# Sparse heads of the even attention: the selection mask is added to the bias bands by GpSimd, not by sixteen products with the identity

## The chip, the cores and the metric

The kernel runs on one core of a Trainium2 chip. The metric is the device time of one execution in microseconds, the median of three runs. Engines: PE is TensorE, DVE is VectorE, ACT is ScalarE, POOL is GpSimd, SP is SyncE, which here only issues weight transfers. PSUM is the memory TensorE writes into, SBUF the memory all engines read; GpSimd doesn't touch PSUM in this kernel.

## The reference

Two transformer blocks of two layers each run in turn over 256 tokens of width 1024. The second block's layer 0 is the "even" layer. Its mixer has two kinds of heads: four differential heads (eight softmaxes) and eight sparse heads, called DSA, which may only see the 64 keys that an index score ranks highest for each query:

```python
    act = jax.nn.relu(jnp.einsum('bqhd,bsd->bqhs', qi, k_idx))
    score = jnp.einsum('bqhs,bqh->bqs', act, wi)
    score = jnp.where(adm[None], score, -jnp.inf)
    _, sel = lax.top_k(score, topk)                     # topk = 64
    ...
    bias = table_a[t5_bucket(sel - tpos[None, :, None])]
    s = jnp.einsum('bqhl,bqkl->bqkh', ql, c_sel) * scale + bias
    s = jnp.where(valid[..., None], s, NEG_INF)
    p = jax.nn.softmax(s, axis=2)
```

The kernel does not gather keys. It computes the scores against all keys and makes the excluded ones so large (the scores are kept negated, so "large" is 1e30) that their exponential is zero. One selection per query serves all eight sparse heads.

## The kernel before

**Tiling.** Tokens lie in two tiles of 128 queries (`qt` 0 and 1). Under the causal limit a query tile 0 sees 128 keys and a query tile 1 sees 256. A "unit" is one head and one query tile. The even layer has 32 units, taken in eight steps `s` of four (two heads by two query tiles): steps 0 to 3 are the differential heads ("joint"), steps 4 to 7 the sparse ones.

**What a unit goes through.** TensorE multiplies queries and keys into PSUM (`scores`). VectorE adds the head's bias band, writes the result to SBUF and takes the row minimum in the same instruction (`biased`, two records on VectorE). ScalarE takes the exponential and its sum. For the differential heads VectorE then combines two softmaxes (`joined`). TensorE transposes the weights (`turn`), VectorE or ScalarE copies them out of PSUM (`copied`), and TensorE multiplies them with the values. Every engine follows a fixed written order and semaphores: `at_s` says that a unit's scores are there, `at_t` that its bias is added, `at_e` that its exponential is done, `at_joint`, `at_x`, `at_yd` and `at_ya` follow for joining, transposing and copying, `at_o` for the values.

**How the mask gets in.** VectorE ranks the index scores in eight rounds of "eight largest" and "replace them" per query tile (`top_rounds`); the last line writes a bf16 tile `sel`, 1e30 where a key is not selected, 0 elsewhere, and counts `sel_ready`. TensorE adds `sel` to the scores of a sparse unit in PSUM by a second product, identity times `sel` (line 1847). Only these second products count `at_s`, so VectorE may not start on any unit of a sparse step before all its query-key products have been issued.

**Around it.** While steps 0 to 3 run, TensorE also computes the last 200 columns of the layer's input projection (`in2_half`, 128x200 products), whose weights VectorE and ScalarE split in two parts (`whi`, a cast by ScalarE, line 2152; `wlo`, a subtraction by VectorE, line 2737). At step 6 VectorE takes the differential heads' output (`diff_out`, `diff_total`, lines 3461 to 3470) and GpSimd normalises it (lines 1042 to 1058).

**Memory.** `band` is the first 4096 columns of `region`, 16 heads by 256 columns; the even layer uses 12. `proj[:, :, 640:1152]` held the index queries, which are dead once they have been transposed; so is `qiT`, `region[:, 3072:4096]`, once the index scores are computed.

Of the kernel before, what the change touches and what calls it, by code (L numbers as in the profile page):

```python
# [204 lines left out]
def build_network(nc, a, out):  # L205
# [66 lines left out]
    with ExitStack() as ctx:  # L272
# [29 lines left out]
        sel = sb("sel", [P, 3 * P], BF16)  # L302
# [19 lines left out]
        cand = region[:, 7040:7296], work[:, 2560:2816]  # L322
# [147 lines left out]
        sel_ready = sem("sel_ready")  # L470
        diff_taken = sem("diff_taken")
# [32 lines left out]
        def unit(qt, slot, w, parts, bias, pv, o_bank, o_col, sel_mask=None):  # L504
            return dict(qt=qt, slot=slot, w=w, parts=parts, bias=bias, pv=pv, o_bank=o_bank, o_col=o_col, sel=sel_mask)
# [19 lines left out]
        def head_unit(qt, q, k, nk_of, bias, v, slot, o, masked):  # L525
            nk = nk_of(qt)
            return unit(qt, slot, nk, [(0, nk, q(qt), k(nk))], bias(qt, nk), [v(s) for s in range(nk // P)], *o(qt),
                        sel[:, (0, P)[qt]:(0, P)[qt] + nk] if masked else None)
# [18 lines left out]

        def even_heads():
            hs = []
            for i in range(2 * HB):  # L550
# [3 lines left out]
                           lambda s, i=i: proj[:, s, 2248 + P * (i // 2):2248 + P * (i // 2) + P], i, out_at(P * (i // 2)), False))  # L554
            return hs

        def dsa_heads():
            hs = []
            for i in range(HA):
                b = half(i)  # L560
                hs.append((lambda qt, i=i, b=b: qT[b:b + 64, 8 + i // 2, qt * P:qt * P + P],
                           lambda nk, i=i, b=b: qT[b:b + 64, 12 + i // 2, 0:nk], causal, band_of(i),
                           lambda s, i=i: proj[:, s, HD * i:HD * i + HD], 2 * HB + i, out_beside(i), True))
            return hs

        def odd_heads():
            hs = []
            for i in range(HC):
# [3 lines left out]
                           lambda s, kv=kv: proj[:, s, 1152 + HD * kv:1152 + HD * kv + HD], i, out_columns(i), False))  # L572
            return hs

        def cross_heads():
            hs = []
            for i in range(HX):
# [3 lines left out]
                           lambda s, i=i: kvn[:, s, 256 + HD * i:256 + HD * i + HD], i, lambda qt, i=i: (6 + qt, P * (i // 2)), False))  # L581
# [341 lines left out]
        def _(pool):  # L923
# [105 lines left out]
            for l in range(DEPTH):  # L1029
# [86 lines left out]
        def _(pe):  # L1116
# [259 lines left out]
            def attention_steps(key):  # L1376
# [3 lines left out]
                def scores(i):  # L1380
# [18 lines left out]
                    for (c0, n, q, k), (c1, _, q1, k1) in zip(pair[0][1]["parts"], pair[1][1]["parts"]):  # L1399
                        m0 = nc.tensor.matmul(scores_of(*pair[0])[:, c0:c0 + n], q, k, start=True, stop=pair[0][1]["sel"] is None)  # L1400
                        m1 = nc.tensor.matmul(scores_of(*pair[1])[:, c1:c1 + n], q1, k1, start=True, stop=pair[1][1]["sel"] is None)
                    if pair[0][1]["sel"] is not None:
                        m0, m1 = [nc.tensor.matmul(scores_of(u, d), ident_b[:], d["sel"], start=False, stop=True) for u, d in pair]
# [107 lines left out]
            for _ in range(WARM):  # L1511
                nc.tensor.matmul(ps[:, 0, :], sel[:, 0:P], sel[:, 0:P].unsqueeze(1).to_broadcast([P, 4, P]), start=True, stop=True)
# [211 lines left out]
            for l in range(DEPTH):  # L1724
# [97 lines left out]
                if even:  # L1822
# [8 lines left out]
                    def scores(s):  # L1831

                        fours = [(u0 + 4 * s + j, us[4 * s + j]) for j in range(4)]
                        for qt in range(TT):
# [1952 lines left out]
```

## Time and profile before

| | |
|---|---|
| time, median of 3 runs | 1346.65 us (1346.65 to 1347.08) |
| span of the profiled execution | 1344.9 us |
| median minus span (start and end around it) | 1.75 us |
| busy in the span: PE, DVE, ACT, POOL | 1334.0, 974.7, 740.4, 124.2 us |
| the last ranking result is written | 788.7 us after the span's start |
| sparse steps, first scores to last values | 799.3 to 817.2 us |
| sixteen products with the identity | 800.2 to 809.5 us |

The times of rows are microseconds from the span's start. The profiled execution gives durations and their order; its span is 1.75 us shorter than the median of the timed runs, so a difference worked out in the trace is added to the median. The timeline lists an instruction's start and duration; consecutive instructions on an engine overlap a little (an end is drawn after the next start), so what one costs its engine is best read from start to start.

### The profile page before, as it was taken

What the parts mean: (1) busy time and instruction counts of PE and PEld (TensorE: products, weight loads), DVE (VectorE), ACT (ScalarE), POOL (GpSimd) and SP (SyncE); (2) the same over time, 40 slices, a digit from 0 to 9 for tenths busy, and PEclk for the clock granted to TensorE, in tenths of its full rate; (3) what the DMA queues carried; (4) which work ended last, traced back from release to release, by engine and by line L of the source; (5) the groups of instructions that cost most, each with busy time, mean ns of one, the idle gap of its engine ahead of it and who ended that gap; (6) DMA issues with size and microseconds to landing.
All of it is one profiled execution on the core that took longest, in us unless ns stands there. A gap on an engine that the chain in (4) does not pass through costs nothing.

```text
span 1344.9 us, 19217 instructions
## 1 busy us (share of the span) xinstructions
PE 1334.0 (99%) x7365; PEld 1121.8 (83%) x7365; DVE 974.7 (72%) x1502; ACT 740.4 (55%) x1155; POOL 124.2 (9%) x114
## 2 busy tenths in 40 slices
PE   9999999999999999999999999999999999999998
PEld 6888888888888888888888777888888878888886
DVE  7566878777664767877778787886667887786665
ACT  6564555454545754555455676754445675654443
POOL 1000011111000000311111002220000011400000
PEclk9999999999999999999999999999999999999999
DMA  9743545555455334667655523357765524355552
GB/s 374 247 151 131 188 157 190 189 193 194 173 219 188 125 126 161 227 200 232 202 190 198 172 95 149 119 217 223 218 206 191 183 79 173 122 203 193 191 190 89
DMA packets 37673, 244.32 MB, mean 182 GB/s; under 512 B 4656, under 2 KB 5312, under 8 KB 10192
## 3 DMA queue, kind: packets, MB, share of 16 engines
q1 hardware_dynamic: 33568, 228.08, 47.5%
q0 software_dynamic: 3728, 14.82, 4.1%
q8 instruction: 59, 0.97, 0.3%
q14 instruction: 30, 0.25, 0.1%
q10 hardware_dynamic: 288, 0.21, 0.1%
HBM read 241.13 MB, written 1.97 MB: 181 GB/s over the span
## 4 chain that ended last, share of the span: by engine, by line
PE 97%; ACT 1%; DVE 1%; DMA 0%; issue 0%; POOL 0%; ACTq 0%; DVEq 0%
PE ps L1217 19%; PE ps L1155 17%; PE ps L1161 16%; PE ps L1164 16%; PE ps L1224 10%; PE ps L1323 3%; PE ps L1449 2%; PE ps L1418 2%; PE ps L1400 1%; PE ps L2035 1%; PE ps L1265 1%; PE ps L1262 1%; PE ps L1259 1%; PE ps L1577 1%; PE ps L2045 1%; PE ps L1578 1%
## 5 line engine op out<-in xcount | busy, mean ns | idle before, releaser
L2737 DVE TENSOR_TENSOR wlo<-raw,whi 128x1024 fp32r<-128x1024 f32 (+2 forms) x423 | 510.4, 1217 | 264.1 <-ACT whi L2152 263.2
L2152 ACT CAST whi<-raw 128x1024 fp32r<-128x1024 f32 (+1 forms) x431 | 444.5, 1041 | 332.5 <-PE ps L1224 188.5
L1217 PE MATMUL ps<-act,whi 128*128 128x512 f32 x1120 | 266.4, 390 | 0.0
L1217 PEld LDWEIGHTS ps<-act,whi 128*128 128x128 f32 x1120 | 208.4, 188 | 42.2
L1155 PE MATMUL ps<-whi,mhi 128*128 128x512 f32 (+2 forms) x688 | 235.7, 392 | 0.0
L1161 PE MATMUL ps<-wlo,mhi 128*128 128x512 f32 (+2 forms) x688 | 231.1, 385 | 0.0
L1164 PE MATMUL ps<-whi,mlo 128*128 128x512 f32 (+2 forms) x688 | 230.9, 385 | 0.0
L1164 PEld LDWEIGHTS ps<-whi,mlo 128*128 128x128 f32 x688 | 129.3, 188 | 26.3
L1161 PEld LDWEIGHTS ps<-wlo,mhi 128*128 128x128 f32 x688 | 129.2, 188 | 26.0 <-DVE wlo L2737 0.5
L1224 PEld LDWEIGHTS ps<-act,wlo 128*128 128x128 f32 x1120 | 143.6, 191 | 5.5
L1155 PEld LDWEIGHTS ps<-whi,mhi 128*128 128x128 f32 x688 | 125.9, 188 | 23.8 <-issue 2.6
L1224 PE MATMUL ps<-act,wlo 128*128 128x256 f32 x1120 | 145.3, 283 | 0.0
L1155 PE MATMUL ps<-whi,act 128*128 128x512 f32 (+1 forms) x336 | 126.3, 376 | 0.0
L1164 PE MATMUL ps<-whi,act 128*128 128x512 f32 (+1 forms) x336 | 124.1, 369 | 0.0
L1161 PE MATMUL ps<-wlo,act 128*128 128x512 f32 (+1 forms) x336 | 124.0, 369 | 0.0
L1155 PEld LDWEIGHTS ps<-whi,act 128*128 128x128 f32 x336 | 63.3, 188 | 11.6 <-ACT whi L2152 0.8
L1164 PEld LDWEIGHTS ps<-whi,act 128*128 128x128 f32 x336 | 63.3, 188 | 10.9
L1005 POOL TENSOR_TENSOR work<-work 128x512 f32<-128x512 f32 x22 | 48.4, 2199 | 257.8 <-DVE work L3139 250.0
L1161 PEld LDWEIGHTS ps<-wlo,act 128*128 128x128 f32 x336 | 63.4, 189 | 10.1
L939 POOL TENSOR_TENSOR rstd<-ss,small 128x2 f32<-128x2 f32 (+1 forms) x22 | 19.3, 878 | 492.7 <-DVE ss L3289 166.8
L2215 ACT ACTIVATE work<-work,low 128x128 f32<-128x128 f32 (+3 forms) x80 | 40.8, 512 | 28.4 <-DVE low L2831 24.1
L2692 ACT CAST mhi<-work 128x512 fp32r<-128x512 f32 x32 | 19.9, 622 | 66.0 <-DVE work L3739 66.0
(334 smaller groups left out, 1516.2 us busy)
## 6 DMA issues: line engine op xcount, KB each, us to landing
raw<-in_weights SPq DMA_DIRECT2D x210, 1024.0 KB, 4.8
gain_b<-in_norm_g POOLq DMA_DIRECT2D x6, 512.0 KB, 4.1
raw<-in_weights SPq DMA_DIRECT2D x5, 512.0 KB, 6.0
region<-in_b_gate POOLq DMA_DIRECT2D x2, 1024.0 KB, 8.2
o_nat<-in_mem_turned POOLq DMA_DIRECT2D x2, 1024.0 KB, 6.8
region<-band POOLq DMA_DIRECT2D x8, 256.0 KB, 5.0
region<-band POOLq DMA_DIRECT2D x8, 192.0 KB, 6.3
x<-in_x SPq DMA_DIRECT2D x1, 1024.0 KB, 11.9
```

The costliest lines, as they stand in the source:

```text
L1005: nc.gpsimd.tensor_tensor(two(up_as), two(up_a), row, ALU.mult).then_inc(a_scaled, 1)
L1155: nc.tensor.matmul(o, hi[:, kx, rows_], wh[:, k, c0:c0 + w], start=first and h == 0 and k == 0 and (tt == 0 or at[1] == 0), stop=False)
L1161: nc.tensor.matmul(o, hi[:, kx, rows_], wl[:, k, c0:c0 + w], start=False, stop=False)
L1164: mm = nc.tensor.matmul(o, lo[:, kx, rows_], wh[:, k, c0:c0 + w], start=False, stop=final and h == 1 and k == kh - 1 and (tt == 1 or at[1] ...
L1217: nc.tensor.matmul(ps[:, bank0 + f, :], of(whi, h)[:, k, f * P:f * P + P], act2[:, kx].rearrange("p i n -> p (i n)"), start=kx == 0, stop= ...
L1224: mm = nc.tensor.matmul(ps[:, bank0 + f, 0:SEQ], of(wlo, h)[:, k, f * P:f * P + P], act2[:, kx, 0], start=False, stop=kx == KD - 1)
L1323: mm = nc.tensor.transpose(bank[:, j * P:j * P + P], src, ident)
L1418: mm = nc.tensor.transpose(turned(u, d)[:, at:at + P], step_of(1536, u, d)[:, at:at + P], ident)
L1449: mm = nc.tensor.matmul(ps[row:row + HD, d["o_bank"], d["o_col"]:d["o_col"] + P], d["pv"][b], values_of(u, d)[:, b * P:(b + 1) * P], start ...
L2152: nc.scalar.copy(whi[:, m % HL, 0:w], raw[:, n % RAW, h * w:h * w + w]).then_inc(hi_done, 1)
L2215: nc.scalar.activation(step_of(1536, u, d), step_of(0, u, d), ACT.Exp, scale=-1.0, bias=low[:, d["qt"], s:s + 1], accum_out=den[:, d["qt"] ...
L2737: nc.vector.tensor_tensor(wlo[:, m % HL, 0:w], raw[:, n % RAW, h * w:h * w + w], whi[:, m % HL, 0:w].bitcast(F32), ALU.subtract).then_inc( ...
```

## The change

The tile `sel` is gone. VectorE writes the mask as f32 into dead parts of `region` (`out_of_top`). GpSimd, whose queue holds nothing between the norm of the latent keys and the wait for `diff_taken`, adds it to the eight sparse heads' bands: for query tile 0 into a copy in the dead part of `proj` (two instructions of four heads by 128), for query tile 1 in place in `band` (four instructions of two heads by 256). VectorE reads these masked bands in `biased`, with one more wait, `masked_ready`. TensorE's second products go, and each query-key product now counts `at_s` itself. The constant tile of the warm-up products at the program's start gets a name of its own, `warm`.

```diff
-        sel = sb("sel", [P, 3 * P], BF16)
+        warm = sb("warm", [P, P], BF16)
...
-        cand = region[:, 7040:7296], work[:, 2560:2816]
+        cand = region[:, 7040:7168], work[:, 2560:2816]
+        out_of_top = region[:, 7168:7296], region[:, 3072:3328]
...
+        def first_masked(h0, n=1):
+
+            return proj[:, h0 // 4, 640 + P * (h0 % 4):640 + P * (h0 % 4 + n)]
+
+        def masked_of(h):
+            return lambda qt, nk: band[:, h, :] if qt else first_masked(h)
...
                     root(("ckv", l), 2)
+
+                    pool.wait_ge(sel_ready, TT * (l // 2) + 1)
+                    for h in (0, 4):
+                        nc.gpsimd.tensor_tensor(first_masked(h, 4).rearrange("p (h n) -> p h n", n=P), band[:, h:h + 4, P:SEQ],
+                                                out_of_top[0].unsqueeze(1).to_broadcast([P, 4, P]), ALU.add).then_inc(masked_ready, 1)
+                    pool.wait_ge(sel_ready, TT * (l // 2) + 2)
+                    pool.wait_ge(masked_ready, (HA // 2 + 2) * (l // 2) + 2)
+                    for h in range(0, HA, 2):
+                        pair = band[:, h:h + 2, :]
+                        nc.gpsimd.tensor_tensor(pair, pair, out_of_top[1].unsqueeze(1).to_broadcast([P, 2, SEQ]), ALU.add).then_inc(masked_ready, 1)
...
                             pe.wait_ge(at_t, u0 + 4 * s - (0 if qt or not s else 2))
-                            mms = []
                             for u, d in pair:
                                 (_, _, q, k), = d["parts"]
-                                mms.append(nc.tensor.matmul(scores_of(u, d), q, k, start=True, stop=d["sel"] is None))
-                            if pair[0][1]["joint"]:
-                                for mm in mms:
-                                    mm.then_inc(at_s, 1)
-                        if not fours[0][1]["joint"]:
-                            for u, d in fours:
-                                nc.tensor.matmul(scores_of(u, d), ident_b[:], d["sel"], start=False, stop=True).then_inc(at_s, 1)
+                                nc.tensor.matmul(scores_of(u, d), q, k, start=True, stop=True).then_inc(at_s, 1)
...
-                    pe.wait_ge(sel_ready, TT)
...
+                    if d["pair"] is not None and not d["joint"]:
+                        dve.wait_ge(masked_ready, (HA // 2 + 2) * (key[1] // 2) + (2 + d["pair"] - HB + 1 if d["qt"] else (d["pair"] - HB) // 2 + 1))
...
-                        nc.vector.tensor_scalar(sel[:, (0, P)[qt]:(0, P)[qt] + nk], c, SENTINEL / 2, BIG, ALU.is_gt, ALU.mult).then_inc(sel_ready, 1)
+                        nc.vector.tensor_scalar(out_of_top[qt], c, SENTINEL / 2, BIG, ALU.is_gt, ALU.mult).then_inc(sel_ready, 1)
```

On TensorE, at the first two sparse steps (4 and 5), the queue before holds the query-key products (`ps<-qT`), the mask products (`ps<-sel,ident_b`) and the transposes of steps 2 and 3 (`ps<-cst,work`):

```order
L1841 MATMUL ps<-qT 128x128 [waits at_t,sel_ready]
L1841 MATMUL ps<-qT 128x128
L1841 MATMUL ps<-qT 128x256 [waits at_t]
L1841 MATMUL ps<-qT 128x256
L1847 MATMUL ps<-sel,ident_b 128x128 x2
L1847 MATMUL ps<-sel,ident_b 128x256 x2
L1428 MATMUL ps<-cst,work 128x128 [waits at_ya,at_joint] x2
L1428 MATMUL ps<-cst,work 128x128
L1841 MATMUL ps<-qT 128x128 [waits at_t,ev_act]
```

and after the change:

```order
L1856 MATMUL ps<-qT 128x128 [waits at_t]
L1856 MATMUL ps<-qT 128x128
L1856 MATMUL ps<-qT 128x256 [waits at_t]
L1856 MATMUL ps<-qT 128x256
L1444 MATMUL ps<-cst,work 128x128 [waits at_ya,at_joint] x2
L1444 MATMUL ps<-cst,work 128x128
L1856 MATMUL ps<-qT 128x128 [waits at_t,ev_act]
```

The four mask products of the step are gone, and the transposes follow the scores directly; nothing else moves on TensorE.

On GpSimd, between the norm of the latent keys (`rstd<-ss,small`) and the squares of the differential heads' output (`o_nat<-o_nat`), the queue before is:

```order
L1027 DMA work<-in_ev_a_w_uk 128x4x128
L1028 DMA work<-in_ev_a_w_uv 128x8x64
L939 TENSOR_TENSOR rstd<-ss,small 128x2 [waits ss_ready]
L1042 TENSOR_TENSOR o_nat<-o_nat 128x512 [waits diff_taken] x2
L1048 COPY work<-rden 128x512 [waits at_x,dsa_weights]
```

and after the change:

```order
L947 TENSOR_TENSOR rstd<-ss,small 128x2 [waits ss_ready]
L1048 TENSOR_TENSOR proj<-region 128x512 [waits sel_ready]
L1048 TENSOR_TENSOR proj<-region 128x512
L1054 TENSOR_TENSOR region<-region 128x512 [waits masked_ready,sel_ready]
L1054 TENSOR_TENSOR region<-region 128x512 x3
L1060 TENSOR_TENSOR o_nat<-o_nat 128x512 [waits diff_taken] x2
L1066 COPY work<-rden 128x512 [waits at_x,dsa_weights]
```

Six additions stand ahead of the squares, behind the transfers of that part. On VectorE the order of the instructions is the same; the sixteen sparse `biased` instructions each have one wait more.

## Rows read from the trace of the kernel before

**Rows 1.** The page's first part: engine, busy us (share) x instructions.

```profile
PE 1334.0 (99%) x7365; PEld 1121.8 (83%) x7365; DVE 974.7 (72%) x1502; ACT 740.4 (55%) x1155; POOL 124.2 (9%) x114
```

**Rows 2.** Windows: length, busy PE, PEld, DVE, ACT, POOL, granted clock, DMA, GB/s.

```profile
794.86:805.24 10.38, 10.18 (x90) 8.45 (x89) 8.68 (x43) 10.38 (x40) 0.00 (x0) 1.00 0.01 2
805.24:812.17 6.93, 5.66 (x55) 4.11 (x54) 6.61 (x28) 5.56 (x19) 5.03 (x6) 1.00 0.00 1
812.17:840.00 27.83, 27.82 (x160) 23.00 (x161) 18.41 (x22) 15.54 (x23) 2.22 (x3) 1.00 0.45 170
```

**Rows 3.** Line 1847, the mask products: durations, and who waited for them.

```profile
L1847 PE MATMUL ps<-sel,ident_b x16: 219/251/273, 800.2 to 809.3; 128*128 128x128 bf16 x8, 128*128 128x256 bf16 x8
...
  DVE work L2831: 0.9, 1
```

**Rows 4.** Timeline of PE, steps 4 to 7: start, duration, engine, line, [idle before].

```profile
799.31 0.93 PE L1841 MATMUL ps<-qT 64*128 64x128 f32 x8
800.17 0.51 PE L1847 MATMUL ps<-sel,ident_b 128*128 128x128 bf16 x4
800.51 0.49 PE L1428 MATMUL ps<-cst,work 128*128 128x128 f32 x3
801.09 1.30 PE L1841 MATMUL ps<-qT 64*128 64x128 f32 x8
...
812.17 0.88 PE L1418 MATMUL ps<-cst,work 128*128 128x128 f32 x6 [1.18 <-ACT work L2215]
```

**Rows 5.** Timeline of ACT where its unbroken stretch begins.

```profile
794.86 0.40 ACT L2215 ACTIVATE work<-work,low 128x128 f32<-128x128 f32 x1 [0.41 <-DVE low L2831]
```

**Rows 6.** Timeline of DVE, from step 5's exponentials to the copy of step 5.

```profile
805.27 0.20 DVE L3497 RECIPROCAL rden<-den 128x8 f32<-128x8 f32 x1 [0.27 <-ACT work L2215]
...
811.25 0.45 DVE L3470 TENSOR_SCALAR small<-small 128x4 f32<-128x4 f32 x1
811.62 0.41 DVE L2878 COPY work<-ps 128x256 f32<-128x256 f32 x1
```

**Rows 7.** Timeline of POOL: additions and products of the sizes added.

```profile
806.50 2.04 POOL L1042 TENSOR_TENSOR o_nat<-o_nat 128x512 f32<-128x512 f32 x2 [57.47 <-DVE o_nat L3462]
...
810.64 1.04 POOL L1058 TENSOR_TENSOR o_nat<-o_nat,small 128x512 f32<-128x512 f32 x1
```

**Rows 8.** Timeline of POOL and DVE where both read two SBUF operands.

```profile
1107.26 1.30 POOL L1076 TENSOR_TENSOR mlo<-o_nat,mhi 128x512 fp32r<-128x512 f32 x1 [0.81 <-ACT mhi L2547]
1107.67 0.91 DVE L3530 TENSOR_TENSOR rden<-den,small 128x16 f32<-128x16 f32 x1
```

**Rows 9.** Timeline of POOL in the first block, the longest of line 1005.

```profile
208.97 3.42 POOL L1005 TENSOR_TENSOR work<-work 128x512 f32<-128x512 f32 x1 [8.85 <-DVE work L3139]
```

**Rows 10.** Timeline of DVE, from the last ranking round to step 0's joining.

```profile
788.69 0.29 DVE L3397 TENSOR_SCALAR sel<-work 128x256 bf16<-128x256 f32 x1
789.00 0.57 DVE L2737 TENSOR_TENSOR wlo<-raw,whi 128x400 fp32r<-128x400 f32 x1
...
790.60 0.15 DVE L3487 TENSOR_TENSOR small<-small 128x1 f32<-128x1 f32 x1
...
792.25 0.29 DVE L2831 CUSTOM_DVE_ANT_0 work<-ps,region 128x128 f32<-128x128 f32 x1 [1.30 <-PE ps L1841]
...
793.56 0.22 DVE L2813 SCALAR_TENSOR_TENSOR rden<-den,small,rden 128x2 f32<-128x2 f32 x1
793.82 0.75 DVE L2816 SCALAR_TENSOR_TENSOR work<-work,rden 128x128 f32<-128x128 f32 x2
```

**Rows 11.** Timeline of DVE from the first mask on.

```profile
772.31 0.23 DVE L3397 TENSOR_SCALAR sel<-region 128x128 bf16<-128x128 f32 x1
...
772.96 0.48 DVE L3379 SCALAR_TENSOR_TENSOR work<-region,proj,work 128x256 f32<-128x256 f32 x1
...
777.28 0.58 DVE L2737 TENSOR_TENSOR wlo<-raw,whi 128x400 fp32r<-128x400 f32 x1 [1.27 <-ACT whi L2152]
```

**Rows 12.** Timeline of ACT: the index scores of the last head pair.

```profile
776.11 0.66 ACT L2459 ACTIVATE region<-ps 128x256 f32<-128x256 f32 x2 [1.78 <-DVE work L3379]
```

More of the change, by code:

```diff
@@ L470, in build_network @@
         sel_ready = sem("sel_ready")
+        masked_ready = sem("masked_ready")
         diff_taken = sem("diff_taken")
@@ L501, in y2b, with unit @@
             return 6 * c + tt
-        def unit(qt, slot, w, parts, bias, pv, o_bank, o_col, sel_mask=None):
-            return dict(qt=qt, slot=slot, w=w, parts=parts, bias=bias, pv=pv, o_bank=o_bank, o_col=o_col, sel=sel_mask)
+        def unit(qt, slot, w, parts, bias, pv, o_bank, o_col):
+            return dict(qt=qt, slot=slot, w=w, parts=parts, bias=bias, pv=pv, o_bank=o_bank, o_col=o_col)
         def half(i):
@@ L523, in dilated_units, with head_unit @@
             return us
-        def head_unit(qt, q, k, nk_of, bias, v, slot, o, masked):
+        def head_unit(qt, q, k, nk_of, bias, v, slot, o):
             nk = nk_of(qt)
-            return unit(qt, slot, nk, [(0, nk, q(qt), k(nk))], bias(qt, nk), [v(s) for s in range(nk // P)], *o(qt),
-                        sel[:, (0, P)[qt]:(0, P)[qt] + nk] if masked else None)
+            return unit(qt, slot, nk, [(0, nk, q(qt), k(nk))], bias(qt, nk), [v(s) for s in range(nk // P)], *o(qt))
         def out_at(col):
@@ L561, in dsa_heads @@
                 hs.append((lambda qt, i=i, b=b: qT[b:b + 64, 8 + i // 2, qt * P:qt * P + P],
-                           lambda nk, i=i, b=b: qT[b:b + 64, 12 + i // 2, 0:nk], causal, band_of(i),
-                           lambda s, i=i: proj[:, s, HD * i:HD * i + HD], 2 * HB + i, out_beside(i), True))
+                           lambda nk, i=i, b=b: qT[b:b + 64, 12 + i // 2, 0:nk], causal, masked_of(i),
+                           lambda s, i=i: proj[:, s, HD * i:HD * i + HD], 2 * HB + i, out_beside(i)))
             return hs
@@ L571, in odd_heads @@
                            lambda nk, kv=kv, b=b: qT[b:b + 64, 8 + kv, 0:nk], causal, band_of(i),
-                           lambda s, kv=kv: proj[:, s, 1152 + HD * kv:1152 + HD * kv + HD], i, out_columns(i), False))
+                           lambda s, kv=kv: proj[:, s, 1152 + HD * kv:1152 + HD * kv + HD], i, out_columns(i)))
             return hs
@@ L1399, in scores @@
                     for (c0, n, q, k), (c1, _, q1, k1) in zip(pair[0][1]["parts"], pair[1][1]["parts"]):
[L1400 to L1403, printed above, removed]
+                        m0 = nc.tensor.matmul(scores_of(*pair[0])[:, c0:c0 + n], q, k, start=True, stop=True)
+                        m1 = nc.tensor.matmul(scores_of(*pair[1])[:, c1:c1 + n], q1, k1, start=True, stop=True)
                     m0.then_inc(at_s, 1)
@@ L1511, in _ @@
             for _ in range(WARM):
-                nc.tensor.matmul(ps[:, 0, :], sel[:, 0:P], sel[:, 0:P].unsqueeze(1).to_broadcast([P, 4, P]), start=True, stop=True)
+                nc.tensor.matmul(ps[:, 0, :], warm[:], warm[:].unsqueeze(1).to_broadcast([P, 4, P]), start=True, stop=True)
             def turn_bias():
@@ L2707, in _ @@
             n_link = [0]
-            nc.vector.memset(sel[:, 0:P], 1.0).then_inc(warm_set, 1)
+            nc.vector.memset(warm[:], 1.0).then_inc(warm_set, 1)
             def mark(ins):
```

4 lines of the change are left out of this document (2 added, 2 removed).

## The prediction

> **What bounds the kernel now.** The first part of the page says that TensorE is busy 99% of the span [rows 1], so it looks as if every product taken away were a gain. That is an average. The change acts between 772 and 817 us, so I cut that stretch into windows [rows 2]. From 794.86 to 805.24 ScalarE is busy 10.38 of 10.38 us: it has no idle time at all, while it takes the exponentials of steps 2 to 5, copies weights and casts. TensorE is also drawn as busy there, 10.18 us, but with the timeline beside it one sees products that stretch over a wait: eight query-key products take 0.93 us at 799.31 and 1.30 us at 801.09 [rows 4]. From 805.24 to 812.17 TensorE is busy only 5.66 of 6.93 us, ScalarE 5.56, VectorE 6.61. From 812.17 on TensorE is full again, 27.82 of 27.83 us. The clock is 1.00 in all three windows, the upper of its two levels (2.4 GHz), with no fall that the change could cause or cure.
>
> So three links set the time at which TensorE becomes full. ScalarE's unbroken stretch starts at 794.86 when VectorE delivers the first biased scores of step 2, after 0.41 us of idle [rows 5]. Its end, the exponentials of step 5, releases VectorE at 805.27, after 0.27 us of idle [rows 6]. VectorE then works without a gap through the shares, the differential heads' output and steps 6 and 7, and comes to the copy of step 5's weights at 811.62, which ends at 812.03 [rows 6]. TensorE, idle for 1.18 us, starts the transposes of step 6 at 812.17 [rows 4]. The trace puts that wait down to the exponentials, which end last; but the transposes of step 6 need step 6's exponentials, long done, and the copy of step 5, because its PSUM place is reused. I take the copy as the releaser.
>
> **The sixteen products, removed.** They are drawn with 0.25 us each [rows 3], but four of them take 0.34 us from start to start (800.17 to 800.51 [rows 4]). Four steps make 4 x 0.34 = 1.36 us of TensorE. Two groups lie in the ScalarE window: TensorE is earlier, ScalarE is not, since it has no idle time to give back. VectorE no longer waits 0.9 us for the first group [rows 3] because it may start at the first query-key product; it finishes its part of step 4 sooner and has its results wait in front of ScalarE. The other two groups, of steps 6 and 7, lie in the second window, where VectorE has 0.32 us of idle in all and 0.27 of it is the wait for ScalarE. TensorE reaches the transposes of step 6 earlier and waits there longer, some 1.18 + 1.36 us less what other waits take. I cost the removal at 0. The cover is ScalarE first and VectorE second; without both it would be worth at most 1.36 us plus part of the 0.9 us.
>
> **The six additions, added.** 128x512 f32 takes GpSimd 1.02 to 1.04 us when a tile is squared or is multiplied with a broadcast one [rows 7], and 1.30 us with two different full inputs [rows 8]. The longest such instruction, its waits included, took 3.42 us [rows 9]. The first pair starts after 772.3 + 0.2 us, the other four after 788.7 + 0.3 = 789.0 us, the end of the last mask [rows 10, 11]. At 1.30 us the four end near 789.6 + 5.2 = 794.8. Nobody needs them before step 4's units of query tile 1, some 800 us, and one pair of heads is needed per step, the last at about 810 us. Even at 3.42 us the pairs would come at 792.4, 795.9, 799.3 and 802.7, each before its step. GpSimd itself was idle for 57.47 us up to 806.50 [rows 7], so its later work is not late either. As work, the additions cost 0.
>
> **What they do to VectorE.** Here I expect the price. At 1107.67 VectorE's 128x16 tensor_tensor with two SBUF inputs took 0.91 us while GpSimd was at a 128x512 subtraction from 1107.26 to 1108.56, and ended 0.02 us behind it [rows 8]. At 811.25 a 128x4 tensor_scalar took 0.45 us, to 811.70, under GpSimd's multiplication from 810.64 to 811.68 [rows 6, 7]. Instructions that small take 0.15 us elsewhere [rows 10]. So some VectorE instructions wait for the end of GpSimd's. In the other direction GpSimd's 3.42 us from 208.97 shows that it waits too [rows 9].
>
> The Trainium skill ("SBUF — State Buffer", section "SBUF: two separate sides") says that a VectorE instruction with two SBUF inputs or in a two-port mode and a GpSimd instruction hold a shared port pair exclusively, whichever starts first, and that the other "fully blocks". These rows agree with it. By that rule the steps' `biased` instructions, with one input in PSUM, would not wait.
>
> In the first part, the index sums (two SBUF inputs, 0.48 us each) follow the first mask directly [rows 11]. One of them held up by an addition is up to 1.3 us late, and two up to 2.1. VectorE's idle 1.27 us before 777.28 does not absorb that, because it comes from a ScalarE cast behind relus, and these wait for the index sums in turn [rows 11, 12]. What does absorb it is the 1.30 us that VectorE waits for step 1's scores at 792.25 [rows 10]; of ScalarE's slack 0.41 us is shown [rows 5]. Bounds: 0 to 2.1 us late at 789, 0 to about 1 us of it left at 794.86. I take 0.2.
>
> In the second part, the `wlo` subtraction keeps the port until 789.57 [rows 10]. With additions of 1.04 us and room for VectorE's tiny instructions at 790.60, the four end at 794.0; with 1.30 us they end at 795.1. Step 0's joining at 793.56 and 793.82 has two SBUF inputs in each instruction [rows 10], and step 2's scores are biased behind it in the queue. If only the first must wait, it loses 794.0 - 793.56 = 0.44 us; if the second waits for the last addition, 795.1 - 793.82 = 1.3 us. Below, the delay could be 0, if VectorE gets in between; above, each of the joinings of steps 0 and 1 waits once, 2.5 us. I take the middle of the two worked cases, rounded down, 0.8. Since ScalarE has nothing to give back after 794.86, and VectorE nothing after 805.27, a delay there comes through whole.
>
> **Small edits.** Sixteen waits more on VectorE: a unit that waits for two semaphores already follows its neighbour without a gap, so 0; if each took 0.05 us (my guess, a third of the smallest instruction above), eight of them in the second link would be 0.4. The mask in f32 instead of bf16 is one instruction of 0.23 and one of 0.29 us [rows 10, 11]: 0, at most as much again. The wait for `sel_ready` on TensorE was met 10 us before: 0. The warm-up tile: 0.
>
> **Sum.** 0 (products) + 0 (additions) + 0.2 + 0.8 (VectorE behind GpSimd) + 0 (small edits) = +1.0 us. The profiled execution goes from 1344.9 to 1345.9 us of span; with the 1.75 us that lie around it the time is 1347.65 us.
>
> **Rivals.** (a) *The additions fall into gaps, nothing moves.* For it: VectorE is idle 1.30 us before 792.25, and its `biased` instructions ran at their usual 0.28 us beside GpSimd at 807. Against it: the joinings lie where the last addition must be. Time 1346.65, between 1346.4 and 1346.9.
> (b) *TensorE really was the bound, and the products were worth their time.* For it: TensorE's 99%, and a drawn wait can be another thing than it seems. Against it: ScalarE's 10.38 of 10.38 us. Then 1346.65 - 1.36 = 1345.3 us, with all of the 0.9 us 1344.4.
> (c) *Serial alternation, the case that is clearly slower.* GpSimd and VectorE take turns, so each joining instruction of steps 0 and 1 (six with two SBUF inputs) waits for an addition and the index sums do too. The price: the four additions' full 4 x 1.3 = 5.2 us minus the 1.30 and 0.41 us of idle, so +3.5 us: 1350.1. It decides once more than two additions lie between step 0's first joining instruction and step 2's scores. Against it: at 208.97 it was GpSimd that waited, so VectorE's consecutive instructions can keep the port [rows 9].
>
> **Chances.** Forecast (delay of 0.3 to 2.5 us) 0.50, (a) 0.25, (b) 0.15, (c) 0.08, something unforeseen 0.02. A measurement of this kernel can tell about 0.2%, 2.7 us, from no change: below 1343.95 is faster, above 1349.35 slower. The forecast, (a) and (b) all lie within. Slower comes from (c) and the forecast's edge, 0.08; faster only from the unforeseen, 0.02; the same 0.90. The range, 1345.2 to 1349.3, takes in the forecast with its bounds, (a), and the nearer half of (b), and leaves out the rest of (b) and (c), some 0.17.
>
> **What would show it.** Right: ScalarE's unbroken stretch starts later than 794.86 (about 795.9) and keeps its length of 10.4 us; VectorE's joining of step 0 is drawn with instructions several times as long as 0.22 and 0.38 us, ending with a GpSimd addition; TensorE's idle before the transposes of step 6 grows from 1.18 us to over 2. For (a), the same instructions keep their lengths. For (b), TensorE starts those transposes before 812. For (c), the stretch starts after 797. I am wrong in kind if step 4's first `biased` instruction waits for GpSimd, or if ScalarE shows idle time between steps 2 and 5.

## The result and the profile after

The changed kernel takes 1348.26 us (median of 21 runs, 1347.74 to 1350.47), the kernel before 1346.81 us (median of 21, 1346.39 to 1347.84) on the same chip. The ratio is 1.0013, interval [1.0007, 1.0019]: some 1.5 us slower, really so, yet less than the 0.2% taken here as no change. The forecast was 1347.65 us. In nearly every kernel here, the one before too, some executions are 1 to 3 us longer than the rest; in the two such ones that were profiled, "copies twice" and "last addition last", the delay is there at 136 us already, far ahead of the change, and its cause is open. Engines of the page of after:

```profile
PE 1332.6 (99%) x7349; PEld 1120.7 (83%) x7349; DVE 977.5 (73%) x1502; ACT 740.2 (55%) x1155; POOL 133.2 (10%) x120
```

Against [rows 1] TensorE lost sixteen products and 1.4 us, and its share is still 99%: that number says nothing of the change. VectorE has as many instructions as before and is drawn busy for 2.8 us more. Its timeline shows where; first behind the first mask (start, duration, engine, line, what, [idle before <- releaser]):

```profile
772.82 1.40 DVE L3389 SCALAR_TENSOR_TENSOR work<-region,proj,work 128x256 f32<-128x256 f32 x1
774.25 2.20 DVE L2745 TENSOR_TENSOR wlo<-raw,whi 128x1024 fp32r<-128x1024 f32 x1
...
790.04 0.29 DVE L3407 TENSOR_SCALAR region<-work 128x256 f32<-128x256 f32 x1
790.25 0.57 DVE L2745 TENSOR_TENSOR wlo<-raw,whi 128x400 fp32r<-128x400 f32 x1
...
791.85 0.15 DVE L3497 TENSOR_TENSOR small<-small 128x1 f32<-128x1 f32 x1
...
792.22 0.29 DVE L2841 CUSTOM_DVE_ANT_0 work<-ps,region 128x128 f32<-128x128 f32 x1
...
793.41 0.17 DVE L2820 RECIPROCAL rden<-den 128x2 f32<-128x2 f32 x1
793.61 0.84 DVE L2821 SCALAR_TENSOR_TENSOR rden<-den,small,rden 128x2 f32<-128x2 f32 x1
794.49 1.32 DVE L2824 SCALAR_TENSOR_TENSOR work<-work,rden 128x128 f32<-128x128 f32 x1
794.49 1.71 DVE L2824 SCALAR_TENSOR_TENSOR work<-work,rden 128x128 f32<-128x128 f32 x2
```

(The last two rows are one place, the first instruction of a pair alone and the pair.) GpSimd's timeline of the same time; the last two rows are the third and the fourth addition by themselves:

```profile
772.47 2.90 POOL L1048 TENSOR_TENSOR proj<-region 128x512 f32<-128x512 f32 x2 [22.68 <-DVE region L3407]
790.42 5.23 POOL L1054 TENSOR_TENSOR region<-region 128x512 f32<-128x512 f32 x4 [15.05 <-DVE region L3407]
...
793.15 1.27 POOL L1054 TENSOR_TENSOR region<-region 128x512 f32<-128x512 f32 x1
794.39 1.26 POOL L1054 TENSOR_TENSOR region<-region 128x512 f32<-128x512 f32 x1
```

Read the two engines side by side. The index sum of 0.48 us [rows 11] takes 1.40 us and ends at 774.22; the two additions overlap it and the split's subtraction behind it, which takes 2.20 us where it took 1.23; GpSimd's pair ends at 775.37. The second mask comes at 790.04 instead of 788.69 [rows 10], although this execution stood 0.15 us ahead at the first index mask (772.16, before 772.31 [rows 11]). At 793.61 the joining's small instruction (0.22 us before) takes 0.84 us and ends at 794.45, just after the third addition ends (793.15 + 1.27 = 794.42); the next one (half of 0.75 us before) takes 1.32 us and ends at 795.81, 0.16 us after the fourth ends (794.39 + 1.26 = 795.65). The reciprocal between them keeps its 0.17 us and the biased instructions, with one input in PSUM, their 0.29 us. Both joining waits together are (0.84 - 0.22) + (1.71 - 0.75) = 1.58 us. The Trainium skill ("SBUF — State Buffer", section "SBUF: two separate sides") has exactly this as a rule: two SBUF inputs on VectorE and a GpSimd instruction exclude each other. The trace agrees on who waits for whom. The 128x1 instruction at 791.85 doesn't test it: it falls on the boundary between the first two additions (790.42 + 1.55 = 791.97).

What follows, on ScalarE and TensorE:

```profile
796.44 0.40 ACT L2223 ACTIVATE work<-work,low 128x128 f32<-128x128 f32 x1 [1.27 <-DVE low L2841]
```

```profile
802.43 0.93 PE L1856 MATMUL ps<-qT 64*128 64x128 f32 x8 [0.43 <-ACT proj L2174]
...
809.01 1.30 PE L1856 MATMUL ps<-qT 64*128 64x128 f32 x8 [0.66 <-DVE low L2841]
...
813.40 0.88 PE L1434 MATMUL ps<-cst,work 128*128 128x128 f32 x6 [1.48 <-ACT work L2223]
```

Windows of after from the start of ScalarE's stretch (length, then busy PE, PEld, DVE, ACT, POOL, clock, DMA, GB/s):

```profile
796.44:806.62 10.18, 9.75 (x84) 8.11 (x83) 8.69 (x43) 10.18 (x40) 0.00 (x0) 1.00 0.01 2
806.66:812.84 6.18, 4.49 (x41) 3.02 (x40) 6.04 (x26) 5.06 (x18) 4.59 (x5) 1.00 0.00 1
```

ScalarE's unbroken stretch starts 1.58 us later than in [rows 5] and is 0.20 us shorter than in [rows 2]; the transposes of step 6 start at 813.40, 1.23 us later than in [rows 4]; the span is 1.2 us longer (1346.1 us). From there on nothing is gained or lost. The clock stays at 1.00. With the 0.15 us by which this execution was ahead, it has lost 1.38 us by the transposes, where the medians say 1.45.

### The profile page after: what moved, and what is told of

The parts are those of the page before. It is cut to its first block, busy times and chain, and to the rows that moved or that the text cites. A ratio compares the mean times of both kernels' runs of the same rounds, so it can differ in the third digit from the quotient of the medians.

```text
span 1346.1 us, 19191 instructions
## 1 busy us (share of the span) xinstructions
PE 1332.6 (99%) x7349; PEld 1120.7 (83%) x7349; DVE 977.5 (73%) x1502; ACT 740.2 (55%) x1155; POOL 133.2 (10%) x120
## 4 chain that ended last, share of the span: by engine, by line
PE 97%; ACT 1%; DVE 1%; issue 0%; DMA 0%; POOL 0%; ACTq 0%; DVEq 0%
PE ps L1235 19%; PE ps L1173 17%; PE ps L1179 16%; PE ps L1182 16%; PE ps L1242 10%; PE ps L1341 3%; PE ps L1434 2%; PE ps L1465 2%; PE ps L1418 1%; PE ps L2043 1%; PE ps L1280 1%; PE ps L1283 1%; PE ps L1277 1%; ACT work L2223 1%; PE ps L1593 1%; PE ps L2053 1%
```

## The experiments

All were timed in five rounds, eleven runs each (one kernel twelve). The interval of one such ratio is 0.0009 to either side, 1.2 us, so a single time tells little below that. The conclusions below rest on the lengths and distances of rows in the trace, which repeat within some hundredths, with the median beside them; the second table has these distances.

| kernel | median, us | before, us | ratio |
|---|---|---|---|
| products only | 1346.47 | 1346.91 | 0.9996 [0.9987, 1.0005] |
| additions only | 1348.36 | 1346.91 | 1.0011 [1.0002, 1.0019] |
| first additions later | 1347.19 | 1346.91 | 1.0001 [0.9992, 1.0010] |
| second additions later | 1346.87 | 1346.91 | 0.9998 [0.9989, 1.0007] |
| both later | 1346.42 | 1346.76 | 0.9997 [0.9988, 1.0006] |
| products twice | 1347.12 | 1346.76 | 1.0004 [0.9995, 1.0013] |
| cast moved too | 1347.05 | 1346.76 | 1.0003 [0.9994, 1.0012] |
| before, cast moved | 1347.37 | 1346.76 | 1.0003 [0.9994, 1.0012] |
| copies twice | 1347.94 | 1346.80 | 1.0010 [1.0002, 1.0019] |
| last addition last | 1346.13 | 1346.80 | 0.9995 [0.9986, 1.0004] |
| changed, again (twelve runs, one of them 2684.47) | 1348.18 | 1346.80 | 1.0012 [1.0003, 1.0021] |
| both later, again | 1346.57 | 1346.80 | 0.9999 [0.9990, 1.0007] |

Distances in the traces, in us. Counting from the start of the first mask takes out how late an execution stands as a whole. A is from the first mask to the start of ScalarE's stretch (step 2's first exponential), B from there to VectorE's 128x8 reciprocal behind step 5's exponentials, C from there to VectorE's copy of step 5, D from the first mask to TensorE's transposes of step 6. The last column is D less that of the kernel before.

| kernel | A | B | C | D | against before |
|---|---|---|---|---|---|
| before | 22.55 | 10.41 | 6.35 | 39.86 | |
| changed | 24.28 | 10.22 | 6.18 | 41.24 | +1.38 |
| changed, again | 24.31 | 10.23 | 6.18 | 41.27 | +1.41 |
| products only | 22.55 | 10.22 | 6.17 | 39.50 | -0.36 |
| additions only | 24.27 | 10.23 | 6.25 | 41.31 | +1.45 |
| first additions later | 23.17 | 10.22 | 6.18 | 40.13 | +0.27 |
| second additions later | 22.90 | 10.21 | 6.18 | 39.85 | -0.01 |
| both later | 22.55 | 10.23 | 6.18 | 39.51 | -0.35 |
| both later, again | 22.54 | 10.23 | 6.18 | 39.51 | -0.35 |
| products twice | 22.54 | 10.48 | 6.59 | 40.16 | +0.30 |
| copies twice | 22.55 | 11.73 | 6.17 | 41.01 | +1.15 |
| before, cast moved | 22.59 | 10.41 | 6.35 | 39.91 | +0.05 |
| cast moved too | 22.59 | 10.71 | 6.37 | 40.22 | +0.36 |
| last addition last | 22.59 | 9.83 | 6.35 | 39.32 | -0.54 |

**Products only.** The changed kernel without the additions and their waits; the sparse heads read the plain bands, so the mask is left out.

```diff
-                           ..., causal, masked_of(i),
+                           ..., causal, band_of(i),
-                    pool.wait_ge(sel_ready, TT * (l // 2) + 1)
...
-                        nc.gpsimd.tensor_tensor(pair, pair, ..., ALU.add).then_inc(masked_ready, 1)
-                        dve.wait_ge(masked_ready, ...)
```

> The changed kernel without the six additions and without the sixteen waits for them; the sparse heads read the plain bands, so the selection is left out of the result. Theory (ScalarE, then VectorE, set the time in this stretch; the loss comes from VectorE waiting behind GpSimd's additions): the sixteen products are worth nothing, time equal to before within 0.4 us (ratio 0.9997 to 1.0003), the idle time of TensorE before step 6's transposes grows to about 2 us. Rival (TensorE was the bound, the products were worth their time): 1.4 us faster than before, ratio 0.9990. Rival (the change's loss comes from the earlier start of the biased instructions, not from GpSimd): 1.2 to 1.5 us slower than before.

0.44 us below before by medians. ScalarE where its stretch begins, then TensorE and VectorE near the end of the sparse steps:

```profile
795.00 0.40 ACT L2213 ACTIVATE work<-work,low 128x128 f32<-128x128 f32 x1 [0.41 <-DVE low L2829]
```

```profile
811.95 0.88 PE L1424 MATMUL ps<-cst,work 128*128 128x128 f32 x6 [1.47 <-ACT work L2213]
```

```profile
805.22 0.20 DVE L3495 RECIPROCAL rden<-den 128x8 f32<-128x8 f32 x1 [0.67 <-ACT work L2213]
805.34 0.13 DVE L3459 RECIPROCAL rden<-den 128x4 f32<-128x4 f32 x1
...
811.39 0.41 DVE L2876 COPY work<-ps 128x256 f32<-128x256 f32 x1
```

From the start of ScalarE's stretch to VectorE's first reciprocal are 10.22 us (before 805.27 - 794.86 = 10.41 [rows 5, 6]), from there to the copy of step 5 6.17 (before 811.62 - 805.27 = 6.35). Together 0.37 us are saved of the products' 1.36, neither my 0 nor the whole. In the changed kernel the same two distances are 10.22 (796.44 to 806.66) and 6.18 us (to 812.84).

The 0.19 us of the stretch can be found. In the kernel before, VectorE idles 0.93 us for step 4's mask products, and ScalarE's exponential of step 4 follows its first biased instruction (VectorE, then ScalarE, kernel before):

```profile
800.44 0.29 DVE L2831 CUSTOM_DVE_ANT_0 work<-ps,region 128x128 f32<-128x128 f32 x1 [0.93 <-PE ps L1847]
800.77 0.40 ACT L2215 ACTIVATE work<-work,low 128x128 f32<-128x128 f32 x1
```

It stands 5.91 us behind the start of the stretch, in "products only" 5.83; step 5's first exponential stands 8.14 us behind it, there 7.95. So ScalarE waited some 0.1 us for VectorE at each of these two places, too little to be drawn as idle.

**Additions only.** Before, with six additions that nobody reads: same size, same time, a constant in place of the mask, targets in dead memory.

```diff
+                    pool.wait_ge(sel_ready, TT * (l // 2) + 1)
+                    for h in (0, 4):
+                        nc.gpsimd.tensor_tensor(proj[:, h // 4, 640:1152]..., band[:, h:h + 4, P:SEQ], adm[:, 0:P]..., ALU.add)
+                    pool.wait_ge(sel_ready, TT * (l // 2) + 2)
+                    for h, at in zip(range(0, HA, 2), (3072, 3584, 5632, 6144)):
+                        nc.gpsimd.tensor_tensor(region[:, at:at + 512]..., band[:, h:h + 2, :], adm..., ALU.add)
```

> The kernel before, products and all, plus six GpSimd additions of the same size and at the same two points as in the change, whose results nobody reads. Theory (the additions hold up VectorE's instructions with two SBUF inputs): the whole loss of the change is here too, 1.2 to 1.8 us slower than before, ratio 1.0009 to 1.0014, and the joining of step 0 is drawn with instructions of 0.8 us and more. Rival (the loss comes from the waits for masked_ready or the f32 mask): equal to before. Rival (removed products give back part of what the additions cost): 2.5 us slower or more.

1.45 us above before, the whole loss, with the same lengths at the joining:

```profile
793.73 0.84 DVE L2823 SCALAR_TENSOR_TENSOR rden<-den,small,rden 128x2 f32<-128x2 f32 x1
794.60 1.71 DVE L2826 SCALAR_TENSOR_TENSOR work<-work,rden 128x128 f32<-128x128 f32 x2
```

No wait on `masked_ready` and no f32 mask is in this kernel, so they are not the cause. VectorE's reciprocal and TensorE's transposes:

```profile
806.78 0.20 DVE L3507 RECIPROCAL rden<-den 128x8 f32<-128x8 f32 x1 [0.38 <-ACT work L2225]
```

```profile
813.59 0.88 PE L1428 MATMUL ps<-cst,work 128*128 128x128 f32 x6 [1.19 <-ACT work L2225]
```

All sixteen products are still here, and yet B is as short as without them (10.23 us) and C is 0.10 shorter. So those distances don't need the products gone: ScalarE starts 1.72 us later (24.27 against 22.55), and what it had waited for comes earlier against it (step 4's first biased instruction, at 801.84, stands 5.29 us behind the start of the stretch, before 5.58). Of the 1.72 us only 1.45 arrive at TensorE. Beside the changed kernel (41.24 against 41.31) the products are worth 0.07 us, not the 0.36 that they are worth alone.

**First additions later.** The two additions of query tile 0 wait until the index sums are done.

```diff
                     pool.wait_ge(sel_ready, TT * (l // 2) + 1)
+                    pool.wait_ge(idx_used, HA * (l // 2) + HA)
```

> The changed kernel with the first two additions held until the last index sum is done (about 780 us), where VectorE ranks with one-input instructions. Theory: index sums and the 128x1024 subtraction at 774 keep their usual lengths, the second mask is written 1.35 us earlier, near 788.7; of this the 0.5 to 1.1 us by which step 0's work was late come back, but the second four additions now stand 1.35 us earlier against the joining of step 0 and meet it less: 0.6 to 1.4 us better than the changed kernel, ratio to before 1.0000 to 1.0007. Rival (only the second four additions matter): equal to the changed kernel, ratio 1.0009 to 1.0013. Rival (only the first two matter): equal to before.

**Second additions later.** Each of the four waits until the first scores of step 1, 2, 3 or 4 are there, so that it runs beside the biased instructions.

```diff
                     for h in range(0, HA, 2):
+                        pool.wait_ge(at_s, first_unit["even", l] + 4 * (h // 2 + 1) + 1)
```

> The changed kernel with the last four additions held one by one until the first scores of steps 1, 2, 3 and 4 are there, when VectorE is about to do biased instructions, whose other input is in PSUM. Theory: the joining of step 0 has its usual lengths again (0.22 and 0.38 us) though step 0 itself starts late; ScalarE's unbroken stretch starts near 795.2, ratio to before 1.0001 to 1.0006, and the second cluster of slower times goes if it comes from these four. Rival (only the first two additions matter): equal to the changed kernel, 1.0009 to 1.0013. Rival (the biased instructions are held up as well): slower than the changed kernel, with biased instructions of 0.5 us and more.

**Both later.** Both edits.

> The changed kernel with both moves: the first two additions wait for the last index sum, the last four wait one by one for the first scores of steps 1 to 4. Theory (the loss is made only where an addition meets a VectorE instruction with two SBUF inputs, above all the joining of step 0): no such instruction is held up, the time is that of the kernel without additions, 0.2 to 0.4 us faster than before (ratio 0.9996 to 0.9999). Rival (additions cost something by themselves, or the waits do): no better than with the four alone held back, 0 to 0.1 us from before.

With the first pair later, the index sum and the subtraction have their 0.48 and 1.23 us, the second mask is at 788.87, and the four additions end 1 us sooner. At the joining of step 0 one wait is left, 0.90 us, and the next pair has its 0.74 us (VectorE, then GpSimd, of "first additions later"):

```profile
793.74 0.90 DVE L2822 SCALAR_TENSOR_TENSOR rden<-den,small,rden 128x2 f32<-128x2 f32 x1
794.67 0.74 DVE L2825 SCALAR_TENSOR_TENSOR work<-work,rden 128x128 f32<-128x128 f32 x2
```

```profile
780.13 2.54 POOL L1049 TENSOR_TENSOR proj<-region 128x512 f32<-128x512 f32 x2 [30.02 <-DVE work L3390]
789.24 5.37 POOL L1055 TENSOR_TENSOR region<-region 128x512 f32<-128x512 f32 x4 [6.57 <-DVE region L3408]
```

With only the four spread out, the index sum and the subtraction are held up as in the changed kernel (1.40 and 2.20 us), the second mask is at 790.25, and the joining has its 0.22 and 0.75 us. Still ScalarE's step 2 starts 0.35 us late (A, 22.90 against 22.55): its exponentials of step 0 come late, at 791.27, and from there it runs without a gap, so its own idle times (0.25 and 0.41 us before steps 1 and 2 in the kernel before) are used up. By medians this kernel came a little below the range that I had expected (0.9998, not 1.0001 to 1.0006).

Against "both later" (D), the four at their early time cost 0.62 us, the first pair 0.34, and both together, the changed kernel, 1.73. The sum of the parts is 0.96: the two delays feed each other, because the late mask pushes the four additions from one joining wait to two (0.68 us of waits at the joining with the first pair late, 1.58 with both early). The medians, 1347.19, 1346.87 and 1348.26 against 1346.42, stand in the same order.

"Both later, again" (its TensorE row) has no instruction of VectorE longer than before and the transposes at 811.84, 0.33 us before [rows 4]:

```profile
811.84 0.88 PE L1436 MATMUL ps<-cst,work 128*128 128x128 f32 x6 [1.47 <-ACT work L2225]
```

> The kernel with both groups of additions held back once more, beside the changed kernel on the same chip. Theory (all of the loss is the additions' place in time): 0.2 to 0.5 us faster than before, 1.4 to 2.3 us faster than the changed kernel. Rival (its advantage was the chance of one comparison): within 0.1 us of before.

> The changed kernel once more, beside the one with both groups of additions held back, on the same chip. Expected: 1.2 to 1.9 us slower than before, ratio 1.0009 to 1.0014.

The pair repeats on one chip: 1348.18 against 1346.57, 1.6 us. The placement of the additions is the loss, and what stays when it is cured is the 0.3 us of the products.

**Products twice.** Before, each mask product issued twice, the mask counted double.

```diff
                             for u, d in fours:
+                                nc.tensor.matmul(scores_of(u, d), ident_b[:], d["sel"], start=False, stop=False)
                                 nc.tensor.matmul(scores_of(u, d), ident_b[:], d["sel"], start=False, stop=True).then_inc(at_s, 1)
```

> The kernel before with each of the sixteen products with the identity done twice (16 more products, 1.36 us of TensorE by the start-to-start times). The removal of sixteen gave 0.3 to 0.4 us, not 0. Theory (ScalarE and VectorE set the time, the products only touch it at the edges, where TensorE is just in time): 0.3 to 0.9 us slower than before, ratio 1.0002 to 1.0007; the small slack of TensorE between steps 4 and 6 is used up by then. Rival (TensorE is the bound, and the removal was masked by something else): 1.3 to 1.5 us slower. Rival (products are wholly free): equal to before.

By medians 0.36 us more for sixteen additional products, by the rows 0.30: about the fraction of the other direction. Most of it shows at a place I had not priced, VectorE's second reciprocal of step 6, which needs step 3's values. It starts 0.48 us behind the first one's 805.29, before 0.25, in "products only" 0.12:

```profile
805.77 0.18 DVE L3462 RECIPROCAL rden<-den 128x4 f32<-128x4 f32 x1 [0.28 <-PE ps L1437]
```

**Copies twice.** Before, with ScalarE's four copies of the joined weights done twice, 4 x 0.36 = 1.44 us of ScalarE more.

```diff
+                    if us[4 * s]["joint"]:
+                        spot = (proj[:, 0, 640:1024], ..., region[:, 6016:6400])[s]
+                        nc.scalar.copy(spot, turned_pair(u0 + i, us[i]))
                     nc.scalar.copy(values_of(u0 + i, us[i], True), turned_pair(u0 + i, us[i])).then_inc(at_ya, 1)
```

> The kernel before, with ScalarE doing each of the four 128x384 copies of the differential heads' weights once more, into a place that nobody reads: 4 x 0.36 us by the start-to-start times, all inside its unbroken stretch. Moving a 1.04 us cast off ScalarE gave nothing, so it is open whether ScalarE bounds or only keeps pace. Theory A (ScalarE has no room at all): 1.3 to 1.5 us slower than before, ratio 1.0010 to 1.0011, though relief gives nothing since TensorE and VectorE are as close behind. Theory B (ScalarE only looks full and has hidden room): 0 to 0.6 us slower, ratio at most 1.0004.

By medians 1.14 us of 1.44 come through, by the rows 1.15, between my two theories. The stretch grows by 1.32 us and C shrinks by 0.18, as it does where ScalarE starts late. Loading ScalarE costs most of the load.

**Before, cast moved.** The opposite: one cast of 1.04 us goes from ScalarE's stretch to GpSimd.

```diff
+                        pool.wait_ge(at_s, first_unit["even", l] + 4 * 2 + 1)
+                        nc.gpsimd.tensor_copy(whi[:, m % HL, 0:w], raw[:, n % RAW, 0:w]).then_inc(hi_done, 1)
...
                         if s == 2:
-                            split_half(n0)
+                            n_split[0] += 1
```

> The kernel before, products and all, with only the 128x1024 cast given to GpSimd at step 2. Theory: ScalarE is relieved, but TensorE with its products of steps 4 and 5 (0.68 us) is now the bound at the values of step 3: 0 to 0.3 us faster than before, ratio 0.9998 to 1.0000, so the products are worth 0.5 to 1.0 us once ScalarE is relieved and the additions are placed well. Rival (the products are free whatever ScalarE does): as fast as the changed kernel with the cast moved.

Nothing gained: +0.6 us by medians, inside the interval, and +0.05 by the rows. The stretch keeps its 10.41 us; ScalarE has gaps in it now, behind VectorE:

```profile
797.58 0.40 ACT L2228 ACTIVATE work<-work,low 128x128 f32<-128x128 f32 x1 [0.42 <-DVE low L2846]
...
800.83 0.40 ACT L2228 ACTIVATE work<-work,low 128x128 f32<-128x128 f32 x1 [0.40 <-DVE low L2846]
```

The second is the exponential of step 4, which waits for VectorE and that for the mask products. So ScalarE was not the one bound of that stretch. It, VectorE and TensorE are late together: load on one costs most of the load, relief of one gives little.

**Cast moved too.** "Both later" with that cast on GpSimd and the additions in the slots of steps 1, 3, 4 and 5.

```diff
+                        if h == 2:
+                            high_by_pool()
+                        pool.wait_ge(at_s, first_unit["even", l] + 4 * (h // 2 + 1 + (h > 0)) + 1)
```

> The changed kernel with its additions held back as in the other two, and besides the 128x1024 cast of the output projection's first weights (1.04 us of ScalarE, in the middle of its unbroken stretch) given to GpSimd, which does it at step 2; the additions for steps 5, 6 and 7 each move one step back. Theory (ScalarE's unbroken stretch sets the time of steps 2 to 5): the stretch gets up to 1.0 us shorter, then TensorE, whose values of step 3 VectorE needs next, becomes the bound after 0.3 to 0.6 us: 0.3 to 0.6 us faster than the same kernel with the cast on ScalarE, 0.5 to 1.0 us faster than before (ratio 0.9992 to 0.9996). Rival (ScalarE only looks full): no gain from the cast, equal to the kernel with both additions held back. Rival (GpSimd's cast meets VectorE's joinings): slower than it.

A miss, 0.6 us slower than "both later". The scores of step 5 are there early, so the last addition follows the third at once and runs over step 3's joining, 1.64 us instead of 0.75:

```profile
800.00 2.64 POOL L1071 TENSOR_TENSOR region<-region 128x512 f32<-128x512 f32 x2 [1.37 <-PE ps L1873]
```

```profile
801.54 1.64 DVE L2843 SCALAR_TENSOR_TENSOR work<-work,rden 128x128 f32<-128x128 f32 x2
```

**Last addition last.** The same, but the fourth addition waits for the sparse heads' joint shares, behind all joinings.

```diff
+                        if h < 6:
+                            pool.wait_ge(at_s, ...)
+                        else:
+                            pool.wait_ge(dsa_weights, 2 * (l // 2) + 1)
```

> The changed kernel, additions held back and the cast given to GpSimd, but the last addition (heads of step 7) only starts once the shares are taken at about 805.3 us, not in a row with the third, where it met the joining of step 3 (2.64 us for two in a row, 0.85 us lost). Theory (the loss there was the port and nothing else): no joining is held up, and with ScalarE relieved and the products gone 0 to 0.3 us faster than both additions held back alone, 0.3 to 0.7 us faster than before (ratio 0.9995 to 0.9998). Rival (the cast by GpSimd costs something itself): slower than before. Rival (ScalarE alone is the bound): 1.0 us faster than with both additions held back, 1.4 faster than before.

```profile
806.25 1.27 POOL L1074 TENSOR_TENSOR region<-region 128x512 f32<-128x512 f32 x1 [3.81 <-DVE rden L3529]
```

All joinings have their lengths of before. 1346.13 us is the lowest median of the study, 0.67 us under before; the ratio's interval still holds 1, but the rows say 0.54 us at the transposes (D, 39.32 against 39.86). B is 9.83 us, where moving the cast alone left it at 10.41 and taking the products alone made it 10.22. Against "both later" it is 0.40 us shorter, and C is 0.17 longer. With the products gone, the cast is worth 0.19 us (39.32 against 39.51 of "both later"); with them in place it was worth nothing.

## Why the prediction was right, and where not

**The mechanism and the place: right.** GpSimd's additions hold VectorE's two-input instructions; "additions only" has the whole loss, "both later" has none. Step 4's biased instructions don't wait for GpSimd. ScalarE's stretch starts late (796.44, where I said about 795.9), and 1.38 of its 1.73 us come through.

**The second part, 0.8 us: 1.58.** I let the four additions start at 789.0 and end between 794.0 and 795.1, and took the middle of "one joining instruction waits" and "the next waits for the last". They ran from 790.42 to 795.65, and both waits came. The term that was mis-sized is this one, and the reason lies in the next: where the mask is on time, in "first additions later", the term measures 0.68 us at the joining.

**The first part, 0.2 us: right as a term, wrong as a picture.** Counted from the first mask, the second comes 1.50 us late, the wait of 1.30 us for step 1's scores takes up most [rows 10], and the joining starts 0.20 us late (793.61 against 793.56, and 0.15). But I let only VectorE's delay meet that cover. The additions wait for the mask, not for the scores, so they took the whole of it along, into the joining. Two terms that I had added were one chain. And the first part has a second way that I left out: "second additions later" shows it costing 0.34 us through ScalarE's late exponentials of steps 0 and 1.

**The products, 0: 0.36 alone, 0.07 in the changed kernel.** The cover that I named, ScalarE's 10.38 of 10.38 us, was not tight: it held two waits of 0.1 us behind VectorE and the mask products. Behind it, TensorE had been just in time for step 3's values: VectorE's two reciprocals stand 0.12 us apart instead of 0.25, and 0.17 to 0.18 us are saved up to the copy. But "additions only" has nearly all of this with the products in place, so in the changed kernel it is the later start that is absorbed, and my sentence that a delay at 794.86 comes through whole is what was wrong. Rival (b) had the full 1.36, almost four times what the products gave alone.

**Rival (c), the turns: right in kind, wrong in price.** I had argued against it. Yet the index sum, the subtraction and the two joining instructions of step 0 each waited for one addition, in turn. It cost 1.45 of the 3.5 us, because only two additions were unfinished when step 0's first joining instruction came, and none was left for step 1's joining, whose 0.22 and 0.75 us are those of before.

**Additions as work, waits, f32 mask, warm tile, 0 each: right.** The additions took 1.26 to 1.30 us where nothing stood in their way, as the upper of my two row values [rows 8]; no sparse step waited for one. (The second of the four times that I worked out with 3.42 us is 795.8, not 795.9; nothing hangs on it.)

**The releaser of step 6's transposes: right.** From the end of VectorE's copy of step 5 to the transposes there are 0.14 us before (811.62 + 0.41 to 812.17 [rows 4, 6]), 0.15 in "products only" (811.39 + 0.41 to 811.95) and 0.15 after (812.84 + 0.41 to 813.40), while the trace names ScalarE each time.

**TensorE's idle before them: wrong.** I expected over 2 us and it was 1.48, from 1.18. The time of the mask products was not saved up for that wait; 0.43 us stand before the scores of step 5, which wait for ScalarE's copy out of PSUM, and 0.66 before those of step 7, which wait for VectorE's biased instructions.

**The sum.** From the first mask, the changed kernel's stretch starts 1.73 us late (0.20 and 1.58, less some hundredths), and 0.35 us of that are gone by the transposes: 1.38 us in the trace, 1.45 by the medians. Of the 0.35, "additions only" has 0.27 (1.72 to 1.45), which leaves 0.07 for the products. The forecast of 1.0 got near partly by luck: 0.78 us of joining too little and 0.35 us of absorption left out stand against each other.

Open: why C shrinks less with the additions alone (6.25 us) than with the products gone (6.18), which is where the 0.07 us lie.

## What to carry to other kernels

Work moved to an idle GpSimd costs by when it runs: each addition holds VectorE's instructions with two SBUF inputs until it ends, so put it where VectorE reads PSUM, and hold it there with a semaphore that fires at that place. Check the new start times of moved work after each delay that it causes, since it may push itself onto the next victim. An engine drawn 100% busy between neighbours as late as itself is a bound for load (1.15 of 1.44 us), not for relief (0 of 1.04 for ScalarE, 0.36 of 1.36 for TensorE, 0.54 with both relieved). Don't add the worth of a relief to the price of a delay: both draw on the same small waits, and here the relief shrank from 0.36 to 0.07 us.

## What the runs showed of the hardware

GpSimd's 128x512 f32 addition with a broadcast operand took 1.26 to 1.30 us undisturbed. The first of four took 1.55, begun while VectorE's subtraction of two SBUF tiles, 790.25 to 790.82, was still at work: GpSimd waits as well. The turns fall one by one. VectorE's joining instruction waited for the third addition and ended 0.03 us behind it, and yet the fourth had begun at 794.39, before VectorE's next one at 794.49; so a row of additions without a gap held up VectorE's two instructions one after the other. An instruction that had waited ended 0.03 or 0.16 us behind the addition, although alone it takes 0.22 or 0.38 us: part of its length passes within the wait.

Some instructions of VectorE outside PSUM were not held up beside an addition: in "first additions later" the 128x256 MAX8 and MATCH_REPLACE8 between 780.13 and 782.67 keep their 0.43 and 0.41 us, and in the changed kernel the 128x2 reciprocal at 793.41 its 0.17.
